# Down products of six-tile chunks from seven block products in place of eight, feed-forward chunks of 6, 6, 6 and 4 tiles

## The chip, the core and the metric

The kernel runs on one core of a Trainium2 chip. The core has a matrix engine (TensorE, PE in the profile, with its weight loads as PEld), a vector engine (DVE), a scalar engine (ACT), GpSimd (POOL), a sync engine (SP) and 16 DMA engines. Each engine works through its own list of instructions in order; they meet at semaphores. The metric is the time of one execution in microseconds. Before the change the median of three runs is 2139.5 us (2136.0 to 2141.06).

## What is computed

A streaming encoder step: 512 new frames of one stream and 64 of another (576 tokens, width 1024) pass through two layers. Each layer has a half-step feed-forward part, a mixer (a gated convolution in layer 0, chunked attention in layer 1) and a second half-step feed-forward part, each behind its own RMS norm; a last norm ends it. There are thus four feed-forward parts:

```python
D_MODEL = 1024; SEQ = 512; DEC_SEQ = 64; D_FF = 2816
def swiglu(x, w_gate, w_up, w_down):
    return (jax.nn.silu(x @ w_gate) * (x @ w_up)) @ w_down
...
for l in range(DEPTH):
    xp = xp + 0.5 * swiglu(rmsnorm(xp, ffn1_norm[l]), ffn1_w_gate[l], ffn1_w_up[l], ffn1_w_down[l])
    # mixer: conv_mixer (l = 0) or attn_mixer (l = 1), plain residual add
    xp = xp + 0.5 * swiglu(rmsnorm(xp, ffn2_norm[l]), ffn2_w_gate[l], ffn2_w_up[l], ffn2_w_down[l])
```

All data are 32-bit floats.

## The kernel before

**Layout.** Activations lie transposed: features on the 128 partitions (8 tiles of 128 for width 1024, 22 for the hidden width 2816), 576 tokens along the free axis, cut into two halves of 288. One matrix instruction multiplies a 128x128 weight tile with 288 tokens. Each operand is split into a high and a low part (`w_hi`, `w_lo` and so on), and a product takes three instructions: hi by hi, hi by lo, lo by hi.

**Phases.** The program is a list of phases (`Plan`, L93). A feed-forward part has chunks of 8, 8 and 6 hidden tiles. The first chunk is a `first` phase, which has an early stretch of plain products (`early`, PE L1403, matrix instructions at L1393) and a late stretch (`late`, L1422, matrix instructions at L1383); a later chunk is a `next` phase (`groups`, L1466). Both form gate and up tiles two by two from seven block products P1 to P7 in place of eight (Strassen's scheme in Winograd's form): j is the group of one gate and one up tile. After each chunk the hidden tiles are multiplied with the down weights: `down` (PE L1525, matrix instructions at L1500), or `last` (L1530) after the last chunk, which also prepares the next norm. There, each of the eight output tiles takes all k tiles of the chunk, 3 instructions each, for both halves: k x 6 instructions.

**Weights.** SP loads raw weight pieces from HBM into 14 staging units; POOL adds a second piece to some of them by accumulating DMAs (`add_pairs`, L610); DVE makes two further sums per group (`add_weights`, L997; instructions at L1001 and L1005). A batch of two pieces is then copied to `w_hi` by ACT (`split_batch`, instruction at L663) and its remainder made in `w_lo` by DVE (L992). There are four batch slots: batch b is split when batch b-4 has been used up, at a place that the plan fixes in the order of ACT (`split_hi`, L646) and of DVE (`split_lo`, L988).

**Order by semaphores.** `run_done` counts finished products. The fifth and sixth operand of a group start in PSUM from a copy (`seed`, ACT, L695), are read by ACT in between (`take_u2`, `take_u4`) and by DVE at the end (`take_c21`, `take_c22`, L1061 and L1056). `xadd_done` counts additions to the residual x (L1212 for a whole tile, L1217 for a half), which free PSUM banks. In `early` ACT copies each plain product out of one of four banks (L718, L721). In `last` the tiles 5, 6, 7 are made as halves (first h0, then h1), so that the norm of the first half is found while PE makes the second: squares, sums, a matrix instruction with ones (L1400), root, reciprocal (L1015), multiplication (L1027).

Of the kernel before, what the change touches and what calls it, by code (L numbers as in the profile page):

```python
# [23 lines left out]
FFN_CHUNKS = (8, 8, 6)  # L24
# [14 lines left out]
PIECE = KQ * P  # L39
W_SLOTS = 4  # L40
# [4 lines left out]
assert sum(FFN_CHUNKS) == FT  # L45

# [16 lines left out]

class Phase:
# [3 lines left out]
    def __init__(self, kind, n, k, **more):  # L68
# [8 lines left out]
        self.adds = []  # L77


class Batch:  # L80
# [4 lines left out]
    def __init__(self, first, second, width, raw, sums, ready):  # L85
        self.first, self.second, self.width, self.raw, self.sums, self.ready = first, second, width, raw, sums, ready


class Plan:
# [3 lines left out]
    def __init__(self):  # L93
        self.phases = []
        for f, norm in enumerate((0, 2, 3, 5)):
            for c, n in enumerate(FFN_CHUNKS):
                self.phases.append(Phase("first" if c == 0 else "next", n, DT, norm=norm, ffn=f, chunk=c))
                if c < len(FFN_CHUNKS) - 1:
                    self.phases.append(Phase("down", DT, n, ffn=f, chunk=c))
# [15 lines left out]
        self.rows = {8: 0, 6: 0}  # L115
# [5 lines left out]
        group = hidden = made = xadds = early = silus = 0  # L121
        for i, p in enumerate(self.phases):
            p.after = self.phases[i + 1] if i + 1 < len(self.phases) else None
            p.before = self.phases[i - 1] if i else None
            p.group, p.hidden, p.made, p.xadds, p.early, p.c11s = group, hidden, made, xadds, early, silus
            p.row = self.rows[p.k]
            self.half_batch = []
            if p.kind in ("first", "conv"):
# [12 lines left out]
                hidden += p.n  # L141
                made += p.n if p.kind == "first" else 0
                self.rows[8] += 2 * groups
                last_set = (groups - 1) % 2
            elif p.kind == "next":
                for kind, j in next_order(0, p.n, None):
                    self.product(p, kind, j, (j + first_set) % 2)
                group += p.n
                silus += p.n
                hidden += p.n  # L150
                made += p.n
                self.rows[8] += 2 * p.n
                last_set = (p.n - 1 + first_set) % 2
            elif p.kind == "down":
                pairs = (0, 1, 2, 4, 5, 6, 0, 1) if last_set == 1 else (4, 5, 6, 0, 1, 2, 4, 5)
                first_set = 1 if last_set == 1 else 0
                for m in range(DT):
                    self.tile(p, ("m", m), pairs[m], p.row + m)
                    self.free_run.append(p.run["m", m])
                xadds += DT  # L160
                self.rows[p.k] += DT
            elif p.kind == "last":
                pairs = (1, 2, 4, 5, 6, 0, 1, 2)
                for m in range(SPLIT_TILE):
                    self.tile(p, ("m", m), pairs[m], p.row + m)
                    self.free_run.append(p.run["m", m])
                for m in range(SPLIT_TILE, DT):
                    self.tile(p, ("h0", m), pairs[m], p.row + m)
# [6 lines left out]
            else:  # L175
                pairs = (4, 5, 6, 0, 1, 2)
                for r in range(3):
                    self.tile(p, ("h0", r), pairs[r], p.row + r)
# [4 lines left out]
                for t in range(1, DT):  # L183
                    for i in range(3 * t, 3 * t + 3):
                        self.tile(p, ("a", i), pairs[i % 6], p.row + i)
# [1612 lines left out]
```

## Time and profile before

| | |
|---|---|
| median of 3 runs | 2139.5 us (2136.0 to 2141.06) |
| the profiled execution, its own time | 2136.56 us |
| its span, first to last instruction | 2134.7 us |
| PE busy | 2088.5 us, 98% |
| DVE busy | 1281.3 us, 60% |
| ACT busy | 944.7 us, 44% |
| granted clock of TensorE | 0.996 of full speed over the span |

The busy times show which engine has least room. The chain of waits that ended last is 86% on PE. A matrix instruction's own duration (near 295 ns) overlaps its neighbours', so what one costs is read from how many start in a stretch.

### The profile page before, as it was taken

Reading aid. Unit: us, or ns where it says so; the run is one execution under the profiler, and the core shown is the slowest. Engines: PE = TensorE matmul, PEld = TensorE weight load, DVE = VectorE, ACT = ScalarE, POOL = GpSimd, SP = SyncE. Lnnn points to the kernel's source line nnn. Section 1 sums busy time; section 2 is a strip of 40 time slices with the busy share of each in tenths; the row PEclk is TensorE's granted clock in tenths of the full one; section 3 lists DMA queues with packets and bytes.
Section 4 is the critical chain, followed back from the end, with each engine's and each line's share of the span. In section 5 each row is a group of like instructions: output and inputs, shape, how many; then the busy total and the mean of one; then the engine's idle time right before and its main releaser. Section 6 shows DMA issues by size and latency. Waiting matters only on the chain.

```text
span 2134.7 us, 37128 instructions
## 1 busy us (share of the span) xinstructions
PE 2088.5 (98%) x15154; PEld 2011.5 (94%) x15154; DVE 1281.3 (60%) x1621; ACT 944.7 (44%) x1597; POOL 201.8 (9%) x259
## 2 busy tenths in 40 slices
PE   8999999999999999999999999999999899999997
PEld 7999999999989999999899999988888889999997
DVE  6745636578566556365764655565655467466465
ACT  5524425456445345154552533543444445244252
POOL 1101000011001010000100100100011001010000
PEclk9999999999999999999999999999999999999999
DMA  7745545457347455444554644422213247365451
GB/s 223 172 116 145 153 100 153 132 145 173 104 133 178 139 130 158 100 123 144 152 165 107 150 144 119 148 91 82 84 57 120 58 133 180 101 159 148 104 144 45
DMA packets 135416, 278.08 MB, mean 130 GB/s; under 512 B 15632, under 2 KB 20032, under 8 KB 135248
## 3 DMA queue, kind: packets, MB, share of 16 engines
q1 hardware_dynamic: 90304, 192.45, 27.7%
q0 software_dynamic: 30976, 57.53, 16.9%
q10 hardware_dynamic: 13968, 25.72, 3.5%
q8 instruction: 122, 2.00, 0.4%
q14 instruction: 46, 0.38, 0.1%
HBM read 268.55 MB, written 7.09 MB: 129 GB/s over the span
## 4 chain that ended last, share of the span: by engine, by line
PE 86%; DVE 6%; ACT 3%; DMA 3%; issue 2%; ACTq 0%; DVEq 0%; POOL 0%; POOLq 0%
PE ps L1383 39%; PE ps L1500 30%; PE ps L1393 7%; PE ps L1636 5%; DMA stage<-w 3%; ACT w_hi L663 2%; DVE w_lo L992 2%; PE ps L1614 1%; DVE neg_max L1283 1%; DVE scores L1280 1%; PE ps L1565 1%; ACT probs L913 1%; PE ps L1596 1%; DVE stage L1001 1%; PE ps L1400 0%
## 5 line engine op out<-in xcount | busy, mean ns | idle before, releaser
L663 ACT ACTIVATE w_hi<-stage 128x1024 fp32r<-128x1024 f32 (+1 forms) x446 | 464.7, 1042 | 614.8 <-PE ps L1500 387.0
L992 DVE TENSOR_TENSOR w_lo<-stage,w_hi 128x1024 fp32r<-128x1024 f32 (+1 forms) x446 | 537.5, 1205 | 284.7 <-ACT w_hi L663 280.8
L1383 PE MATMUL ps<-xa_hi,w_hi 128*128 128x288 f32 x1280 | 379.4, 296 | 2.4 <-ACT u L701 2.4
L1500 PE MATMUL ps<-hid_hi,w_hi 128*128 128x288 f32 x1664 | 380.5, 297 | 0.8 <-DVE hid_lo L1299 0.8
L1500 PE MATMUL ps<-hid_lo,w_hi 128*128 128x288 f32 x1664 | 378.1, 296 | 0.0
L1500 PE MATMUL ps<-hid_hi,w_lo 128*128 128x288 f32 x1664 | 377.9, 296 | 0.0
L1383 PE MATMUL ps<-xa_lo,w_hi 128*128 128x288 f32 x1280 | 377.9, 295 | 0.0
L1383 PE MATMUL ps<-xa_hi,w_lo 128*128 128x288 f32 x1280 | 376.8, 294 | 0.0
L1383 PE MATMUL ps<-xb_hi,w_hi 128*128 128x288 f32 x1200 | 358.4, 299 | 10.8 <-DVE up L1056 6.9
L1383 PE MATMUL ps<-xb_lo,w_hi 128*128 128x288 f32 x1200 | 354.3, 295 | 0.0
L1383 PE MATMUL ps<-xb_hi,w_lo 128*128 128x288 f32 x1200 | 353.2, 294 | 0.0
L1500 PEld LDWEIGHTS ps<-hid_hi,w_hi 128*128 128x128 f32 x1664 | 275.4, 189 | 2.6 <-issue 2.0
L1500 PEld LDWEIGHTS ps<-hid_lo,w_hi 128*128 128x128 f32 x1664 | 275.5, 189 | 0.3
L1500 PEld LDWEIGHTS ps<-hid_hi,w_lo 128*128 128x128 f32 x1664 | 275.4, 189 | 0.0
L1212 DVE SCALAR_TENSOR_TENSOR x<-ps,x 128x576 f32<-128x576 f32 x94 | 71.2, 758 | 311.4 <-PE ps L1500 311.4
L1383 PEld LDWEIGHTS ps<-xa_hi,w_hi 128*128 128x128 f32 x1280 | 240.0, 188 | 3.2 <-ACT u L701 3.0
L1383 PEld LDWEIGHTS ps<-xa_hi,w_lo 128*128 128x128 f32 x1280 | 241.1, 188 | 0.0
L1383 PEld LDWEIGHTS ps<-xa_lo,w_hi 128*128 128x128 f32 x1280 | 240.3, 188 | 0.0
L1383 PEld LDWEIGHTS ps<-xb_hi,w_hi 128*128 128x128 f32 x1200 | 225.0, 187 | 15.7 <-DVE up L1056 9.7
L1383 PEld LDWEIGHTS ps<-xb_hi,w_lo 128*128 128x128 f32 x1200 | 226.1, 188 | 0.0
L1383 PEld LDWEIGHTS ps<-xb_lo,w_hi 128*128 128x128 f32 x1200 | 225.4, 188 | 0.3
L614 POOL DMA_DIRECT2D stage<-w x100 | 86.6, 866 | 1250.2 <-DMA stage<-w 1204.4
(123 smaller groups left out, 2439.7 us busy)
## 6 DMA issues: line engine op xcount, KB each, us to landing
stage<-w SPq DMA_DIRECT2D x460, 256.0 KB, 3.8
stage<-w SPq DMA_DIRECT2D x104, 512.0 KB, 3.9
stage<-w POOLq DMA_DIRECT2D x200, 256.0 KB, 4.9
w_raw<-w ACTq DMA_DIRECT2D x80, 256.0 KB, 3.1
stage<-w SPq DMA_DIRECT2D x32, 384.0 KB, 3.8
x<-x_t SPq DMA_DIRECT2D x8, 288.0 KB, 5.0
k_t<-k_sb ACTq DMA_DIRECT2D x8, 288.0 KB, 2.1
v_t<-v_sb ACTq DMA_DIRECT2D x8, 288.0 KB, 2.5
```

The source lines that it names most:

```text
L614: pool.dma_start(stage[:, s3, :], w8[row][:, 0:PIECE], accum_op=ALU.add).then_inc(pair_added[sum3], 16)
L663: act.activation(prepared(w_hi, b), raw_of(b), ACT.Copy).then_inc(w_hi_done, 1)
L913: act.activation(probs[:, prob_slot(w, t), e, 0:width], scores[:, e, 0:width], ACT.Exp, bias=neg_max[:, w, e:e + 1], scale=1.0, accum_out= ...
L992: dve.tensor_tensor(prepared(w_lo, b), raw_of(b), prepared(w_hi, b).bitcast(F32), ALU.subtract).then_inc(w_ready, 1)
L1001: dve.tensor_tensor(stage[:, base + S2, :], stage[:, s3, :], stage[:, base + A22, :], ALU.add).then_inc(sum_done, 1)
L1212: dve.scalar_tensor_tensor(halves(x[:, m, :]), pair_banks(tile_bank(p, m)), share, halves(x[:, m, :]), ALU.mult, ALU.add).then_inc(xadd_do ...
L1280: dve.tensor_tensor(scores[:, :, 0:width], ps[:, S_BANK:S_BANK + 2, 0:width], bias[:, :, 0:width][:, :, ::-1], ALU.add).then_inc(scores_re ...
L1283: dve.tensor_reduce(neg_max[:, w, :], scores[:, :, 0:width], mybir.AxisListType.X, ALU.max, negate=True).then_inc(neg_max_done, 1)
L1383: mm = pe.matmul(ps[:, bank, 0:HALF], wt[:, b % W_SLOTS, w], xt[:, k, :], start=(start and k == 0 and n == 0), stop=(k == KQ - 1 and n == ...
L1393: mm = pe.matmul(ps[:, bank, 0:HALF], w_raw[:, b % W_SLOTS, w], raw_operand(c)[:, k, :], start=(start and k == 0), stop=(k == KQ - 1), ski ...
L1500: mm = pe.matmul(ps[:, bank + i, 0:HALF], wt[:, b % W_SLOTS, w], xt[:, k, cols(h)], start=(k == 0 and n == 0), stop=(k == p.k - 1 and n == 2))
L1636: mm = pe.matmul(ps[:, bank + i, 0:HALF], wt[:, b % W_SLOTS, w], xt[:, k % KQ, :], start=(k == 0 and n == 0), stop=(k == DT - 1 and n == 2))
```

## The change

The chunks become 6, 6, 6 and 4 hidden tiles. For the three chunks of six, `down` no longer makes eight tiles from six inputs each: inputs are kept as three pairs of tiles with seven operands per pair (B11, T1, B22, T3, T2, T4, B21), each as high and low part, and output tiles are made two by two from seven products of three pairs (9 matrix instructions each). There are four groups j, taken two at a time. The last chunk of four keeps the `last` phase as it was, with four inputs.

```diff
-FFN_CHUNKS = (8, 8, 6)
+FFN_CHUNKS = (6, 6, 6, 4)
+HIDDEN = ("B11", "T1", "B22", "T3", "T2", "T4", "B21")
+DOWN_C = (6, 0, 2, 6)
+DOWN_U = (7, 1, 3, 7)
+DOWN_E = (4, 5, 4, 5)
...
+def down_order(n):
+    order = []
+    for j in range(0, n, 2):
+        for kinds in (("P1", 0), ("P1", 1), ("P7", 0), ("P6", 0), ("P6", 1), ("P7", 1), ("P5", 0), ("P5", 1),
+                      ("P2", 0), ("P2", 1), ("P4", 0), ("P4", 1), ("P3", 0), ("P3", 1)):
+            order.append((kinds[0], j + kinds[1]))
+    return order
...
 # ACT, early: the split that follows the sixth plain product is moved behind two operand copies
-                    split_hi(p.run[kind, j])
+                    if e != 5 or p.n == DT:
+                        split_hi(p.run[kind, j])
...
                     if e == 6:
                         operand_hi(n, 5, diff_done, diffs + 3)
                         operand_hi(n, 6, diff_done, diffs + 4)
+                        if p.n < DT:
+                            split_hi(p.run[early_order(p.n)[5]])
...
 # DVE, down (for each two groups a, a + 1)
-                for m in range(DT):
-                    add_tile(p, m, 0.5)
-                    split_lo(p.run["m", m])
...
+                    for j in (a, a + 1):
+                        split_lo(p.run["P2", j])
+                    if a == 0 and p.chunk == 0:
+                        first_row_lo(p.before)
+                    for j in (a, a + 1):
+                        split_lo(p.run["P4", j])
+                    for j in (a, a + 1):
+                        dve.wait_ge(run_done, p.run["P4", j] + 1)
+                        dve.wait_ge(xadd_done, base + j - a + 3)
+                        add_to_x(x[:, 2 * j + 1, cols(0)], ps[:, DOWN_E[j], 0:HALF], 0.5)
+                    for j in (a, a + 1):
+                        split_lo(p.run["P3", j])
+                    for j in (a, a + 1):
+                        dve.wait_ge(run_done, p.run["P3", j] + 1)
+                        add_to_x(halves(x[:, 2 * j, :]), pair_banks(DOWN_C[j]), 0.5)
...
 # PE, down
+            def down_product(p, kind, j, combo, bank, start):
+                b, half = p.piece[kind, j]
+                c = HIDDEN.index(combo)
+                pe.wait_ge(w_ready, PLAN.batches[b].ready)
+                for q in range(PAIR_TILES):
+                    w = slice(half * DOWN_PIECE + q * P, half * DOWN_PIECE + (q + 1) * P)
+                    hi, lo = pair_ops[:, q, 0, c, :], pair_ops[:, q, 1, c, :]
+                    for n, (wt, xt) in enumerate(((w_hi, hi), (w_hi, lo), (w_lo, hi))):
...
+                    def p1(j):
+                        if j == 1:
+                            pe.wait_ge(c11_done, p.c11s)
+                        elif j == 2:
+                            pe.wait_ge(c12_done, p.c11s)
+                        elif j == 3:
+                            pe.wait_ge(xadd_done, p.xadds + 7)
...
 # PE, next, groups 0 and 1
-                           else pe.wait_ge(xadd_done, p.xadds - 2))
+                           else pe.wait_ge(xadd_done, p.xadds - 8))
```

ACT's `groups` keeps its line: for groups 0 and 1 the seed waits for `xadd_done` at `p.xadds - 1`, one before the last addition of the `down` phase. The operands of a pair are made by DVE (seven per two tiles, in place of two products of gate and up) and copied to their high parts by ACT, and their low parts by DVE.

Two places in the order of instructions. The first is DVE's in the `down` phase after the first chunk, from the sums at its first P2 to the last addition of the first two groups. Before the change, the same phase around its third and fourth output tile:

```order
L1034 TENSOR_TENSOR xa_lo<-xa_raw,xa_hi 128x1152 [waits x_hi_done,run_done]
L1034 TENSOR_TENSOR xa_lo<-xa_raw,xa_hi 128x1152 [waits x_hi_done]
L1212 SCALAR_TENSOR_TENSOR x<-ps,x 128x576 [waits run_done]
L992 TENSOR_TENSOR w_lo<-stage,w_hi 128x1024 [waits w_hi_done]
L1212 SCALAR_TENSOR_TENSOR x<-ps,x 128x576 [waits run_done]
L992 TENSOR_TENSOR w_lo<-stage,w_hi 128x1024 [waits w_hi_done]
```

and with the change:

```order
L1129 TENSOR_TENSOR stage<-stage 128x384 [waits raw_loaded2,pair_added2]
L1133 TENSOR_TENSOR stage<-stage 128x384 [waits raw_loaded5,sum_done]
L1120 TENSOR_TENSOR w_lo<-stage,w_hi 128x768 [waits w_hi_done]
L1162 TENSOR_TENSOR xa_lo<-xa_raw,xa_hi 128x1152 [waits x_hi_done,run_done]
L1162 TENSOR_TENSOR xa_lo<-xa_raw,xa_hi 128x1152 [waits x_hi_done]
L1129 TENSOR_TENSOR stage<-stage 128x384 [waits raw_loaded9,pair_added4]
L1133 TENSOR_TENSOR stage<-stage 128x384 [waits raw_loaded12,sum_done]
L1120 TENSOR_TENSOR w_lo<-stage,w_hi 128x768 [waits w_hi_done]
L1426 SCALAR_TENSOR_TENSOR x<-ps,x 128x288 [waits xadd_done,run_done] x2
L1120 TENSOR_TENSOR w_lo<-stage,w_hi 128x768 [waits w_hi_done]
L1426 SCALAR_TENSOR_TENSOR x<-ps,x 128x576 [waits run_done] x2
```

The addition of a finished result to x (L1212 before, L1426 now) came ahead of the split; now a split stands ahead of the last two additions, and sums and splits stand between.

The second is ACT's in the first `early` stretch, from the last two operand copies on; before the change:

```order
L688 ACTIVATE xb_hi<-xb_raw 128x1152 [waits diff_done] x2
L721 ACTIVATE est<-ps 128x288 [waits run_done]
L656 DMA w_raw<-w 128x512 [waits run_done]
L656 DMA w_raw<-w 128x512
L718 ACTIVATE est<-ps 128x288 [waits run_done]
L721 ACTIVATE est<-ps 128x288 [waits run_done]
L663 ACTIVATE w_hi<-stage 128x1024 [waits sum_done,pair_added2,run_done]
L718 ACTIVATE est<-ps 128x288 [waits run_done]
L721 ACTIVATE est<-ps 128x288 [waits run_done]
L663 ACTIVATE w_hi<-stage 128x1024 [waits sum_done,pair_added0,run_done]
```

and with the change:

```order
L754 ACTIVATE xb_hi<-xb_raw 128x1152 [waits diff_done] x2
L729 ACTIVATE w_hi<-stage 128x1024 [waits sum_done,pair_added2,run_done]
L810 ACTIVATE pair_raw<-ps 128x288 [waits run_done]
L729 ACTIVATE w_hi<-stage 128x1024 [waits sum_done,pair_added0,run_done]
L807 ACTIVATE pair_raw<-ps 128x288 [waits run_done]
L810 ACTIVATE pair_raw<-ps 128x288 [waits run_done]
L729 ACTIVATE w_hi<-stage 128x1024 [waits sum_done,raw_loaded2,run_done]
L810 ACTIVATE pair_raw<-ps 128x288 [waits run_done]
L761 ACTIVATE ps<-pair_raw 128x288 [waits c11_done]
```

Of 16 plain products' copies ten stood ahead of the first split (L663) and twelve ahead of the second; of 12 copies now seven stand ahead of the first (L729) and eight ahead of the second.

## Rows read from the trace of the kernel before

**Rows 1.** The page, busy time, share of the span and instructions of each engine.
```profile
PE 2088.5 (98%) x15154; PEld 2011.5 (94%) x15154; DVE 1281.3 (60%) x1621; ACT 944.7 (44%) x1597; POOL 201.8 (9%) x259
```

**Rows 2.** Windows, third feed-forward part: early, late, down of eight, last; busy us (instructions), clock.
```profile
1009.38:1040.82 31.44, 31.44 (x131) 24.59 (x131) 25.67 (x25) 18.27 (x31) 0.86 (x1) 1.00 0.36 118
1040.82:1106.09 65.27, 64.65 (x483) 64.20 (x482) 48.23 (x61) 36.29 (x58) 8.72 (x10) 1.00 0.73 194
1106.09:1157.27 51.18, 51.18 (x386) 51.18 (x385) 20.73 (x22) 11.29 (x11) 3.70 (x5) 1.00 0.35 86
1366.72:1406.80 40.08, 39.03 (x293) 38.73 (x292) 22.87 (x29) 22.64 (x36) 4.43 (x9) 1.00 0.34 110
```

**Rows 3.** Waits of PE: us in total, times, longest us.
```profile
PE ps L1383 <- DVE up L1056: 6.9, 11, 1.7
PE ps L1383 <- ACT ps L695: 3.9, 8, 0.5
```

**Rows 4.** Groups by line and shape: busy us, mean ns of one, idle before.
```profile
L1217 DVE SCALAR_TENSOR_TENSOR x<-ps,x 128x288 f32<-128x288 f32 x36 | 16.4, 455 | 35.8 <-PE ps L1500 35.8
L1001 DVE TENSOR_TENSOR stage<-stage 128x512 f32<-128x512 f32 x100 | 68.7, 687 | 20.5 <-DMA stage<-w 20.4
L1034 DVE TENSOR_TENSOR xa_lo<-xa_raw,xa_hi 128x1152 fp32r<-128x1152 f32 x24 | 31.6, 1353 | 0.4 <-ACT xa_hi L688 0.4
L992 DVE TENSOR_TENSOR w_lo<-stage,w_hi 128x768 fp32r<-128x768 f32 x32 | 30.6, 957 | 7.6 <-ACT w_hi L663 5.7
L663 ACT ACTIVATE w_hi<-stage 128x768 fp32r<-128x768 f32 x32 | 27.1, 846 | 52.2 <-PE ps L1500 37.8 <-PE ps L1383 14.3
```

**Rows 5.** Timeline, from a down phase to the next chunk: start us, us, engine.
```profile
307.80 1.06 ACT L663 ACTIVATE w_hi<-stage 128x1024 fp32r<-128x1024 f32 x1 [5.34 <-PE ps L1500]
307.80 0.76 DVE L1212 SCALAR_TENSOR_TENSOR x<-ps,x 128x576 f32<-128x576 f32 x1 [4.08 <-PE ps L1500]
308.89 1.23 DVE L992 TENSOR_TENSOR w_lo<-stage,w_hi 128x1024 fp32r<-128x1024 f32 x1 [0.34 <-ACT w_hi L663]
309.39 0.40 ACT L695 ACTIVATE ps<-ps 128x288 f32<-128x288 f32 x1 [0.53 <-PE ps L1383]
309.84 0.40 PE L1383 MATMUL ps<-xb_hi,w_hi 128*128 128x288 f32 x1 [0.48 <-ACT ps L695]
```

**Rows 6.** Timeline of the early stretch of the second feed-forward part.
```profile
612.19 4.04 PE L1393 MATMUL ps<-xa_raw,w_raw 128*128 128x288 f32 x16
616.55 27.32 PE L1393 MATMUL ps<-xa_raw,w_raw 128*128 128x288 f32 x112
634.41 1.06 ACT L663 ACTIVATE w_hi<-stage 128x1024 fp32r<-128x1024 f32 x1 [1.73 <-DVE stage L1001]
637.45 1.06 ACT L663 ACTIVATE w_hi<-stage 128x1024 fp32r<-128x1024 f32 x1 [0.88 <-DVE stage L1001]
638.41 0.39 ACT L718 ACTIVATE est<-ps 128x288 f32<-128x288 f32 x1
643.50 0.51 PE L1383 MATMUL ps<-xb_hi,w_hi 128*128 128x288 f32 x1
```

**Rows 7.** Timeline, ends of two last phases (before the convolution, before attention).
```profile
406.83 0.46 DVE L1217 SCALAR_TENSOR_TENSOR x<-ps,x 128x288 f32<-128x288 f32 x1 [1.55 <-PE ps L1500]
408.41 0.72 PE L1400 MATMUL ps<-sumsq,ones 128*128 128x288 f32 x2
413.31 2.63 DVE L1027 TENSOR_TENSOR xa_raw<-xa_raw,rstd 128x1152 f32<-128x1152 f32 x2
414.73 0.51 PE L1393 MATMUL ps<-xa_raw,w_raw 128*128 128x288 f32 x1
1400.63 0.72 PE L1400 MATMUL ps<-sumsq,ones 128*128 128x288 f32 x2 [1.05 <-DVE sumsq L1011]
```

**Rows 8.** Start of the program: PE's timeline, then windows with the granted clock.
```profile
14.54 4.87 PE L1393 MATMUL ps<-xa_raw,w_raw 128*128 128x288 f32 x12 [3.97 <-DVE xa_raw L1027]
14.00:18.00 4.00, 3.46 (x9) 2.52 (x10) 3.50 (x6) 2.67 (x8) 0.00 (x0) 0.66 0.86 264
```

**Rows 9.** DMA issues: queue, count, KB each, median us to landing.
```profile
stage<-w SPq DMA_DIRECT2D x460, 256.0 KB, 3.8
stage<-w SPq DMA_DIRECT2D x32, 384.0 KB, 3.8
```

More of the change, by code:

```diff
@@ L77, in __init__ @@
         self.adds = []
+        self.paired = kind in ("first", "next") and self.chunk < len(FFN_CHUNKS) - 1
 class Batch:
-    def __init__(self, first, second, width, raw, sums, ready):
+    def __init__(self, first, second, width, raw, sums, ready, piece=None):
+        self.piece = piece
         self.first, self.second, self.width, self.raw, self.sums, self.ready = first, second, width, raw, sums, ready
@@ L98, in __init__ @@
                 if c < len(FFN_CHUNKS) - 1:
[L99 removed]
+                    self.phases.append(Phase("down", DOWN_GROUPS, n, ffn=f, chunk=c))
                 else:
@@ L120, in __init__ @@
         self.sets = 0
-        group = hidden = made = xadds = early = silus = 0
+        group = seeds = pairs = hidden = made = xadds = early = silus = 0
         for i, p in enumerate(self.phases):
@@ L241, in product @@
         base = 7 * part
-        if kind == ("P1" if p.kind == "next" or j >= DT else "P6"):
+        if p.kind == "down":
+            if kind == "P1" and part == 0:
+                self.load_down_pair(p, j)
+        elif kind == ("P1" if p.kind == "next" or j >= DT else "P6"):
             s3 = A11 if kind == "P6" and j // 2 % 2 else S3
@@ L271, in product, with load_down_pair @@
             self.add_piece(p, kind, j, base + piece, sums)
+    def load_down_pair(self, p, j):
+        for piece, row, second in ((A11, 0, 0), (S3, 0, 0), (A21, 1, 0), (A12, 0, 1), (A22, 1, 1)):
+            for part in range(2):
+                self.load_piece(p, 7 * part + piece, 2 * (j + part) + row, second)
+        for kind, piece, second in (("P7", S3, 0), ("P5", A21, 1)):
+            for part in range(2):
+                p.piece["s3", j + part] = S3
+                sums = p.piece.setdefault(("sums", j + part), {})
+                sums[kind] = self.add_second(p, 7 * part + piece, part + (2 + part if kind == "P7" else 0),
+                                             2 * (j + part) + 1, second)
     def tile(self, p, name, pair, row):
@@ L635, in _ @@
             for p in PHASES:
-                if p.kind in ("first", "next", "conv"):
+                if p.kind in ("first", "next", "conv", "down"):
                     add_pairs(p)
@@ L773, in late @@
                     take_c12(j)
+                    if p.kind == "first" and j == p.n - 1:
+                        last_tile_hi(p)
                     split_hi(p.run["P3", j])
@@ new lines, in pair_lo, with tile_lo @@
+            def pair_lo(p, q, first, end, hi, done=1):
+                dve.wait_ge(pair_hi_done, PAIR_HI * (p.pairs + q) + hi)
+                part = flat(pair_raw[:, q, 1, first:end, :])
+                dve.tensor_tensor(flat(pair_ops[:, q, 1, first:end, :]), part,
+                                  flat(pair_ops[:, q, 0, first:end, :]).bitcast(F32),
+                                  ALU.subtract).then_inc(pair_ready, done)
+            def tile_lo(p, j):
+                q = j // 2
+                if not p.paired:
+                    hidden_lo(p, j, up[:, j % 2, :])
+                elif j % 2 == 0:
+                    pair_lo(p, q, 0, 2, 2)
+                else:
+                    pair_lo(p, q, 2, 7, 5, 3)
```

416 lines of the change are left out of this document (306 added, 110 removed).

## The prediction, as it was put on record before the run

> **What bounds the kernel.** I read the busy times first: PE is busy 98% of the span, DVE 60%, ACT 44% [rows 1]. The windows of one feed-forward part say the same by stage: early, late, down and last keep PE busy all through, at full clock, and the waits of PE by releaser are only a few microseconds [rows 2, 3]. So the count of matrix instructions sets the time, and any wait that PE gets anew comes on top.
>
> Two prices on PE. The down of eight has 384 matrix instructions (8 x 8 x 6) in 51.18 us: 0.1333 us each [rows 2]. Plain products: 112 records from 616.55 to 643.50, 0.2406 us each [rows 6], and eight records make one plain product, 1.925 us; a split product of 12 instructions is 1.60 us, a new down product of 9 is 1.20 us.
>
> **A. Down products.** Before, per feed-forward part: 384 + 384 + 6 x 48 = 1056 instructions. After: 3 x 28 x 9 + 4 x 48 = 948. That is 108 fewer, 432 in four parts: **-57.6 us**.
>
> By the Trainium skill (TensorE: Matmul & The Clock Gate, section "Wait — 56ns, not 53.3ns?") back-to-back matmuls at the high clock start N / 2.4 GHz plus 2.5 ns apart, 122.5 ns for 288 columns. The trace has 133.3 ns [rows 2], which decides; with the page's figure A would be an estimated -52.9 us and B +23.5 us.
>
> **B. More split products for gate and up.** Two tiles move from the first chunk to later ones. A tile there has seven split products, in the first chunk two plain and five split ones. Before: 8 x 5 + 14 x 7 = 138 split ones, after 6 x 5 + 16 x 7 = 142: four more per part, 6.4 us, **+25.6 us** in all.
>
> **C. Early stretch, 12 plain products in place of 16.** By count it would take 23.6 us in place of 31.3 (643.50 - 612.19) [rows 6]. But ACT's first two weight splits wait for DVE's sums, which follow the norm's chain on DVE; that chain starts with the stretch and does not get shorter. They ran at 634.41 and 637.45 [rows 6]. Now the ninth product's copy stands behind the second split, and PE's twelfth product needs it. The copy would end where the row's does, at 638.41 + 0.39 = 638.8, PE starts the twelfth at 638.9 and ends at 640.8. Behind the copy ACT has a copy, a split, a copy and the seed, 0.41 + 1.06 + 0.39 + 0.41 less overlaps of 0.09, until 640.9. The late stretch starts at about 641.0, 28.8 us after the start: 2.5 us saved per part, **-10 us**, and not 30.8. Bounds: -30.8, and nothing saved.
>
> **D. A new wait at P1 of group 3.** It needs bank 6, freed by the seventh addition to x. Take PE at 0 when a down starts. P1 of group 3 would start after 15 products, at 18.0. P3 of group 1 ends at 16.8. In front of the seventh addition DVE has a split that waits for this end: 0.20 until ACT starts (307.60 to 307.80), ACT 0.85, DVE 0.96, then the addition 0.76, with an overlap of 0.09 [rows 4, 5]. So it ends no sooner than 19.6: floor 1.6 us. DVE is also behind. From P5's end at 9.6: two u copies and the split on ACT to 10.97, the split on DVE to 11.96, two additions of 0.76 (0.68 each with overlap) to 13.3, two sums of 384 (estimated 0.55 from 0.687 for 512) to 14.4, ACT and DVE split to 15.7, two sums to 16.7; ACT's split waits for the first of these and runs 16.15 to 17.0, DVE's to 18.0, two half additions of 0.455 to 18.75, the split to 19.6, the seventh addition to 20.3. PE waits 2.35 us. After the first chunk two operand remainders of 1.35 us stand in between as well [rows 4]: the same count gives 23.0 and a wait of 5.1 us. Per part 5.1 + 2.35 + 2.35 = 9.8: **+39.2 us**. Behind the waiting P1 all of PE's list stands. Floor 19 us, if DVE has no backlog; above, 60 if the sums wait for loads too.
>
> **E. The seed after a down.** Before, the seed follows P1 of the next chunk and PE waits about 0.65 us (0.48 in the row, the rest start-up of the first instruction) [rows 3, 5]. Now it also waits for the last but one addition, which stands behind a 1024-wide split. From the end of the down: 0.20 + 1.06 + 1.23 + 0.76 + 0.40 and the hand-overs, 3.7 us; DVE's backlog, in which sums wait for a piece whose unit is only then freed, makes it 4.05. PE has P1's 1.60 us to do: wait 2.45. There are three per part in place of two: 3 x 2.45 - 2 x 0.65 = 6.05, **+24.2 us**; floor 20.
>
> **F. End of last.** The last phase now has 24 instructions per tile in place of 36, and 12 per half tile in place of 18. But the chain from the last h0 tile (its end 406.63, the addition at 406.83) through L1400 at 408.41 to the multiplication at 413.31, whose first half ends near 414.67 and releases PE at 414.73 [rows 7], is DVE's and ACT's; h1 tiles of 4.8 us in place of 7.2 no longer fill it. So 2.4 us of A do not arrive, in each of four parts; before attention, where PE already waits 1.05 us for the sum [rows 7], 1.9 more: **+11.5 us**. Bounds 0 and 20.
>
> **G. Late stretch.** For two tiles PE takes 16 us. DVE has five splits of 1.14 (with overlap), four sums, four reads of 0.37 and now the pair's operands: two tiles of 0.76 + 0.76 become 576 + 288 + 576 in the first and 288 + 864 + 288 + 288 + 1440 in the second, some 5.6 us in place of 3.1. That is 15.6 of 16 us. PE waits for DVE's L1056 already, 6.9 us in all [rows 3]. I take 1.5 us more per part, **+6 us**; bounds 0 and 20.
>
> **H. The clock.** Before PE's first plain product it idled 3.97 us, and in 14 to 18 us the granted clock was 0.66 on average, so at its lower level (1.2 of 2.4 GHz) for much of it [rows 8]. I let the four waits of 5.1 us in D do the same, at (1 - 0.66) x 4 = 1.4 us each: **+5.6 us**.
>
> Operands ready at a down's start I cost at nothing: the first products use tiles made earlier, and the last tile's T3 would be ready 2.2 us after the start, against 2.4 needed. Should DVE be late by a microsecond there, twelve downs cost up to 12 us.
>
> **Sum.** -57.6 + 25.6 - 10.0 + 39.2 + 24.2 + 11.5 + 6.0 + 5.6 = +44.5. From the profiled execution's 2136.56 us: **2181 us**. The median of the runs is 2.9 us above that execution, within what I leave open.
>
> **Rivals.**
> - *The additions come in time* (the other side). If DVE reaches the seventh addition before 18.0 and the last but one before the seed is due, D, E and H go: 44.5 - 39.2 - 24.2 - 5.6 plus one more seed of 0.65 per part = -21.9, **2115 us**. It decides at 18.0 after a down's start. For it: DVE is only 60% busy. Against it: the order, split ahead of addition, whose split waits for an end at 16.8. Chance 0.07; if C and F came in full too, the time would be 2077, which I count within these.
> - *Floors.* DVE has no backlog: D 19, E 20, F 7, G and H nothing, which leaves -57.6 + 25.6 - 10 + 46 = +4, **2141 us**. For it: my sums of DVE take each operation one after another. Against: DVE has some 13.8 us of work per 16.8, more after the first chunk. Chance 0.13, a third of it within 0.2%.
> - *Loads late.* Each two groups now take ten loads and four accumulating ones in 16.8 us. A piece of 384 KB lands in 3.8 us, as one of 256 KB does [rows 9]; so pieces of 192 KB hardly land sooner, while the units are freed 7.2 us ahead of use in place of 9.6. If sums then wait 1 to 2 us in each of 24 such stretches: +25 us, **2206 us**. For it: DVE's sums wait 20.4 us for loads already [rows 4]. Against: by my count these land 2 us before they are needed. Chance 0.13.
>
> By the Trainium skill (DMA: Bandwidth & Descriptors, section "Anatomy of one DMA — SWDGE (gpsimd) path") a DMA takes a fixed 2 us plus its bytes at 436 GB/s; the trace's 3.8 us for either size agrees that size hardly counts. By it the third rival would be likelier than I have it.
>
> **Chances.** Forecast 0.67, rivals 0.07, 0.13, 0.13. A measurement of this kernel can tell 0.2%, 4.3 us, from no change. Faster 0.08, same 0.04, slower 0.88. The range from 2146 to 2210 takes the forecast's own bounds, the upper rival and the top of the second's.
>
> **What would show it.** D: PE's wait for DVE's addition line, 12 times, 5 us after first chunks, some 2.4 after others. E: 12 waits for ACT's seed near 2 us in place of 8 of 0.5. C: early stretches of 28 to 29 us, PE waiting on ACT before the twelfth product. F: a wait of near 2 us before the first plain product. A: 432 fewer matrix instructions at 0.133 us. It is wrong if the waits at P1 of group 3 are short, so that PE stays 98% busy.

## The result, and the profile after

The changed kernel takes **2257.65 us** (median of 4 runs, 2252.68 to 2259.15) against 2137.75 us (4 runs, 2134.36 to 2141.06) of the kernel before on the same chip: 1.0552 times as long, 95% interval 1.0531 to 1.0573. The forecast was 2181 us with a range up to 2210: slower, as said, but by 116 us in the spans of the profiled runs (2134.7 and 2250.9) and not by 44.5.

The page after, busy time of each engine, answers to [rows 1]:

```profile
PE 2079.4 (92%) x14786; PEld 1990.8 (88%) x14786; DVE 1564.1 (69%) x2137; ACT 1111.2 (49%) x1905; POOL 285.4 (13%) x355
```

PE is nearly as busy as before (2079.4 against 2088.5 us) with 368 fewer instructions, and its share fell from 98% to 92%. The waits of PE, us in total, times, longest us; before, the two lines of [rows 3] were the seed (3.9 us) and DVE's read in the split groups (6.9 us):

```profile
PE ps L1645 <- DVE x L1426: 39.6, 12, 5.2
PE ps L1623 <- ACT ps L761: 24.5, 12, 2.5
PE ps L1623 <- ACT u_u L775: 21.7, 22, 1.1
PE ps L1633 <- ACT pair_raw L807: 20.6, 4, 6.6
PE ps L1623 <- DVE up L1184: 16.4, 19, 1.7
PE ps L1653 <- DVE sumsq L1139: 14.5, 6, 5.8
PE ps L1633 <- DVE xa_raw L1155: 7.2, 3, 4.0
```

From the top: a down's fourth group (step D), the seed after a down (E), ACT's read of P5's sum, which P3 needs (u4; not in the forecast), the copy of a plain product (C), DVE's read of P7's sum, which P4 needs (c22; G), and the end of a last phase (F, two lines). The windows of the third feed-forward part, the columns as in [rows 2] (busy us and instructions of PE, PEld, DVE, ACT, POOL, then clock, DMA share, GB/s), in the order early, late, down, next, down, next, down, next of four tiles, last:

```profile
1069.20:1099.60 30.40, 25.69 (x98) 19.51 (x99) 25.70 (x25) 16.21 (x26) 0.00 (x0) 0.91 0.29 91
1099.60:1152.80 53.20, 49.97 (x363) 48.78 (x361) 42.25 (x58) 29.36 (x47) 10.42 (x12) 0.99 0.68 163
1152.80:1193.30 40.50, 35.34 (x252) 34.97 (x253) 30.15 (x43) 20.21 (x31) 6.10 (x8) 0.96 0.61 143
1193.30:1265.50 72.20, 68.00 (x507) 67.29 (x506) 54.27 (x73) 38.02 (x59) 10.45 (x12) 1.00 0.60 150
1265.50:1301.40 35.90, 33.53 (x254) 33.30 (x253) 26.68 (x39) 18.27 (x29) 6.93 (x8) 1.00 0.68 159
1301.40:1375.80 74.40, 69.79 (x507) 68.85 (x506) 54.11 (x73) 37.80 (x59) 10.39 (x12) 0.98 0.60 147
1375.80:1411.70 35.90, 33.53 (x254) 33.30 (x254) 25.93 (x40) 18.21 (x29) 6.93 (x8) 1.00 0.66 158
1411.70:1459.20 47.50, 45.02 (x338) 44.79 (x337) 29.59 (x39) 22.45 (x37) 3.45 (x4) 1.00 0.50 130
1459.20:1491.50 32.30, 28.01 (x196) 27.47 (x195) 20.89 (x29) 21.73 (x36) 4.42 (x9) 0.95 0.43 134
```

Two things are to be seen. The helpers have less slack: DVE is busy 25.7 of 30.4 us in early and 42.3 of 53.2 in late, where it was 25.7 of 31.4 and 48.2 of 65.3 [rows 2]. And the granted clock is below 1.00 in five of nine windows, where before it was 1.00 in all four.

For all four parts I added up the distances between PE's first instructions of consecutive stages (the last one up to PE's last instruction), and set the forecast beside them (before, plus the change in the count of instructions times 0.1333 us, plus the terms):

| stage, us over four parts | before | forecast | after | after less forecast |
|---|---|---|---|---|
| early | 127.2 | 117.2 | 124.7 | 7.5 |
| late | 264.7 | 206.7 | 214.4 | 7.7 |
| downs | 409.5 | 448.0 | 459.4 | 11.4 |
| products of later chunks | 633.1 | 746.9 | 788.3 | 41.4 |
| last | 163.4 | 123.7 | 126.8 | 3.1 |

These 71.1 us are the miss, but for some 0.5 outside the four parts. What the low clock costs is counted from the distances between PE's instructions in stretches at the lower level (1.2 of 2.4 GHz), each less what it is at the upper one: 39.4 us after (347 distances) and 2.3 us before (22).

### The profile page after: what moved, and what is told of

Its sections match the earlier page's. It is cut to its first block and busy times, and to the rows that moved or that the text cites. A ratio compares the mean times of both kernels' runs of the same rounds, so it can differ in the third digit from the quotient of the medians.

```text
span 2250.9 us, 38384 instructions
## 1 busy us (share of the span) xinstructions
PE 2079.4 (92%) x14786; PEld 1990.8 (88%) x14786; DVE 1564.1 (69%) x2137; ACT 1111.2 (49%) x1905; POOL 285.4 (13%) x355
## 3 DMA queue, kind: packets, MB, share of 16 engines
q1 hardware_dynamic: 116800, 204.00, 28.8%
## 5 line engine op out<-in xcount | busy, mean ns | idle before, releaser
L1120 DVE TENSOR_TENSOR w_lo<-stage,w_hi 128x1024 fp32r<-128x1024 f32 (+2 forms) x558 | 619.5, 1112 | 371.0 <-ACT w_hi L729 369.4
L729 ACT ACTIVATE w_hi<-stage 128x1024 fp32r<-128x1024 f32 (+2 forms) x558 | 538.1, 967 | 428.3 <-DVE stage L1129 249.1
L683 POOL DMA_DIRECT2D stage<-w x296 | 257.0, 909 | 1614.1 <-DMA stage<-w 1586.6
L1645 PE MATMUL ps<-pair_ops,w_hi 128*128 128x288 f32 x2016 | 416.7, 303 | 39.9 <-DVE x L1426 39.6
L1623 PE MATMUL ps<-xa_hi,w_hi 128*128 128x288 f32 x1344 | 404.5, 301 | 24.7 <-ACT u_u L775 21.7
L1623 PE MATMUL ps<-xb_hi,w_hi 128*128 128x288 f32 x1200 | 363.6, 303 | 40.9 <-ACT ps L761 24.5
L1645 PEld LDWEIGHTS ps<-pair_ops,w_hi 128*128 128x128 f32 x2016 | 333.9, 195 | 44.2 <-DVE x L1426 42.4
L1645 PE MATMUL ps<-pair_ops,w_lo 128*128 128x288 f32 x1008 | 302.6, 300 | 0.0
L1645 PEld LDWEIGHTS ps<-pair_ops,w_lo 128*128 128x128 f32 x1008 | 196.4, 195 | 0.0
L1633 PE MATMUL ps<-xa_raw,w_raw 128*128 128x288 f32 x512 | 136.6, 429 | 27.8 <-ACT pair_raw L807 20.6
L1633 PEld LDWEIGHTS ps<-xa_raw,w_raw 128*128 128x128 f32 x512 | 101.8, 200 | 59.3 <-ACT pair_raw L807 22.4
L1753 PE MATMUL ps<-hid_hi,w_hi 128*128 128x288 f32 x512 | 130.8, 302 | 3.0 <-DVE hid_lo L1278 2.3
```

The source lines that it names most:

```text
L683: pool.dma_start(stage[:, unit, 0:part.stop - part.start], {8: w8, 6: w6}[k][row][:, part], accum_op=ALU.add).then_inc(pair_added[pair_sum ...
L729: act.activation(prepared(w_hi, b), raw_of(b), ACT.Copy).then_inc(w_hi_done, 1)
L1120: dve.tensor_tensor(prepared(w_lo, b), raw_of(b), prepared(w_hi, b).bitcast(F32), ALU.subtract).then_inc(w_ready, 1)
L1623: mm = pe.matmul(ps[:, bank, 0:HALF], wt[:, b % W_SLOTS, w], xt[:, k, :], start=(start and k == 0 and n == 0), stop=(k == KQ - 1 and n == ...
L1633: mm = pe.matmul(ps[:, bank, 0:HALF], w_raw[:, b % W_SLOTS, w], raw_operand(c)[:, k, :], start=(start and k == 0), stop=(k == KQ - 1), ski ...
L1645: mm = pe.matmul(ps[:, bank, 0:HALF], wt[:, b % W_SLOTS, w], xt, start=(start and q == 0 and n == 0), stop=(q == PAIR_TILES - 1 and n == 2 ...
```

## The experiments

Each run is compared with the kernel before on the same chip; medians of before were 2136.7 to 2139.2 us. The gains below are against the changed kernel's 2257.65 us, which was measured apart from them, so a difference under some 5 us says nothing. Waits and stages come from one profiled execution of each run, and can differ by some us from what the medians say. The edits are shown shortened: a line can stand for several of the kernel's. "The clock's cost" is always counted as above.

### Clock: fill

```diff
+ if (kind, j, q, n) == ("P1", 2, PAIR_TILES - 1, 2):
+     fill(bank, 20 if p.chunk == 0 else 9)
+ if j == 0: fill(1, 8)                 # next chunk, ahead of the seeded P6
+ if e == 11 and p.n < DT: fill(5, 20)  # early, ahead of the twelfth plain product
```

> Edit: the kernel after, with matrix instructions of 128 columns on constants that PE issues where it would otherwise idle: 20 ahead of the fourth group's first product in downs after the first chunk (9 in the other downs), 8 ahead of the seeded product of every next chunk, 20 ahead of the twelfth plain product. They are made to be shorter than the wait they fill, so every wait for DVE or ACT ends when it did. Theory (each of these waits also takes TensorE's clock down, and this is the main thing I sized too small): the lower-clock stretches outside the start and the end go, mean clock 0.99, and about 35 us come back: 2222 us. Rival (a fallen clock costs the 5.6 us that I gave it, the rest of the miss is work of ACT and DVE): 2250 us or more.

The first of these stands in the middle of a product, in the same bank on other columns, and x comes out wrong; why was not looked into, and the run counts for its time alone. Measured: **2231.7 us**, ratio 1.0442 (1.0426 to 1.0457), 26 us less; mean granted clock 0.992 in place of 0.974. What the low clock costs fell from 39.4 to 9.0 us. The waits that were filled are no longer shown as idle, and some behind them grew, u4's from 21.7 to 26.7 us and c22's from 16.4 to 19.3:

```profile
PE ps L1628 <- ACT u_u L775: 26.7, 24, 2.4
PE ps L1628 <- DVE up L1184: 19.3, 17, 1.7
PE ps L1628 <- ACT ps L761: 6.0, 12, 2.3
PE ps L1652 <- DVE x L1426: 5.6, 12, 0.7
```

So the clock was a term of 37 us, not of 5.6, and 30 of it are had back by instructions that compute nothing. 26 reach the end of the program.

### Order of DVE in a down: add_first, row, ready_row

```diff
  # add_first: both additions of P3 ahead of the splits at P3
+ for j in (a, a + 1): dve.wait_ge(run_done, p.run["P3", j] + 1); add_to_x(...)
  for j in (a, a + 1): split_lo(p.run["P3", j])
- for j in (a, a + 1): dve.wait_ge(...); add_to_x(...)
```

> Edit: the kernel after, with DVE's two last additions of each pair of down groups ahead of the weight split that they stood behind. Theory: PE's wait at the fourth group's first product (39.6 us in 12) and at the seed after a down (24.5 in 12) nearly go, and with them the clock's falls there, some 25 us: 2170 to 2180 us. Rival (DVE is too busy in a down; the split comes 1.5 us later and PE then waits for weights instead): half of it, 2215 us, with new waits of PE for the remainder line of the weights.

Measured: 2224.3 us, ratio 1.0409 (1.0393 to 1.0424). The waits at the fourth group fell only from 39.6 to 29.2 us, those for the seed to 17.2. My theory was half wrong: the last split was not the only thing ahead of the seventh addition.

```diff
  # row: the operand remainders of the first down
- if a == 0 and p.chunk == 0: first_row_lo(p.before)   # ahead of the splits at P4
+ if a == 2 and p.chunk == 0: first_row_lo(p.before)   # ahead of the splits at P5
```

> Edit: the kernel after, with DVE's two operand remainders (1.35 us each) of the first down moved from ahead of the second products' splits of groups 0 and 1 to the same place of groups 2 and 3, behind their first additions. Theory (after first chunks DVE's backlog is these two): the four waits of 5.1 us at the fourth group's first product become 2.4 us, and the clock falls for half as long: 10.8 + some 4 = 15 us, 2243 us. Rival (the backlog comes from sums that wait for loads, and the remainders fill time that DVE would wait anyway): under 4 us.

Measured: 2255.0 us, ratio 1.0542 (1.0514 to 1.057): nothing that can be told. The longest wait at the fourth group did fall from 5.2 to 2.8 us (30.3 in all), but the seed's rose from 24.5 to 30.2 and u4's from 21.7 to 25.2. By stages the downs fell from 459.4 to 451.0 us and the products of later chunks rose from 788.3 to 796.2: what was taken out of the downs was paid behind them.

```diff
  # ready_row: row, and
  for j in (a, a + 1): split_lo(p.run["P2", j])
+ additions of P4 (a, a + 1); addition of P3 (a)
  for j in (a, a + 1): split_lo(p.run["P4", j])
- additions of P4 (a, a + 1)
+ addition of P3 (a + 1)
  for j in (a, a + 1): split_lo(p.run["P3", j])
- additions of P3 (a, a + 1)
```

> Edit: as the run before, and DVE's last four additions of each two groups stand ahead of the sums and splits at the fourth and third products, each where its data is ready. With only the last two additions ahead of the last split the run of that gave 2224 us and left 29.2 us of waits there, DVE being held by the split that ACT had to do first. Theory (the order of DVE alone makes these waits, it has the time): the waits for the addition line fall below 8 us in 12 and those for the seed below 12, 2185 us. Rival (DVE's time is full in a down: 26.7 of 35.9 us are busy, and the rest is latency that only moves): sums and splits come late instead, and PE waits for weights; 2215 us.

Measured: **2190.5 us**, ratio 1.0237 (1.0193 to 1.0281), 67 us less. The wait for the addition is gone from the list, and the first down of the third part, which had taken 40.5 us, runs without a gap and at full clock, though DVE is still busy 27.9 us in it, against 30.2 (the window's columns as above):

```profile
1122.99:1156.50 33.51, 33.51 (x252) 33.40 (x253) 27.86 (x41) 18.06 (x30) 6.12 (x8) 1.00 0.69 164
```

The twelve downs fell from 459.4 to 399.9 us. So step D, 39.6 us of waits, was 59.5 with what went with it, the clock above all, and all of it came from the order on DVE (row alone had taken 8.4 of it out of the downs and lost it behind them): what it had to take over before the seventh addition was splits that wait for ACT, which waits for sums. The seed's waits stayed, at 25.8 us. In that kernel's successor comb (below) ACT's timeline shows why (start, us, engine, idle before it and what ended that):

```profile
1367.41 2.95 ACT L729 ACTIVATE w_hi<-stage 128x1024 fp32r<-128x1024 f32 x3 [4.37 <-DMA stage<-w]
```

Three splits stand ahead of the seed, and the first waited for a load. In the changed kernel itself it was not so: there ACT's seed waited for DVE's addition all 12 times, 25.1 us in all, as step E says.

### Pair operands: nextu4, next2, thin

```diff
  # nextu4, ACT:  seed, u2, [copy of pair operands moved] c11, u4, + tile_hi(p, j - 1)
  # nextu4, DVE:  splits P6, P2, + tile_lo(p, j - 1), split P5, c22, split P7
  # next2, DVE:   splits P6, P2, P5, c22, + tile_lo(p, j - 1), split P7
```

> Edit: the kernel after, with ACT's copy of the pair operands (up to 128x1440) behind the two reads that PE waits for in the groups of next chunks, and DVE's remainder of it one split later. Theory: PE's waits for the read before the seventh product (21.7 us in 22) fall below 6 us: 2240 us. Rival (DVE's remainder then delays its read before the fourth product, PE's wait of 16.4 us for that line grows by as much): 2255 us.

Measured: 2267.4 us, ratio 1.061 (1.0589 to 1.0631), slower by some 10 us, and by more than the rival had it. Its mechanism held: the waits for u4 fell to 9.6 us, those for c22 rose from 16.4 to 37.8.

> Edit: the kernel after, with ACT's copy of the pair operands behind its reads, and DVE's remainder of it behind DVE's read of the sixth product in place of ahead of it. With the remainder one split later the waits for ACT's read fell from 21.7 to 9.6 us, and those for DVE's read rose from 16.4 to 37.8. Theory (only DVE's place of the remainder made those): waits for both lines together 38.1 us before, now under 20: 2238 us. Rival (the operations of pair operands do not fit into the group whatever their order): 2255 us or more.

Measured: 2247.2 us, ratio 1.05 (1.0478 to 1.0521). Waits for c22 are 21.7 and for u4 6.5 us, 28 together in place of 38. The place of the remainder matters, but 10 us are half of what I expected. What had held PE in the changed kernel is seen where one of those 22 waits is. ACT, then DVE, then PE:

```profile
1224.21 1.06 ACT L729 ACTIVATE w_hi<-stage 128x1024 fp32r<-128x1024 f32 x1 [2.47 <-DVE stage L1129]
1225.18 1.39 ACT L784 ACTIVATE pair_ops<-pair_raw 128x1440 fp32r<-128x1440 f32 x1
1226.47 0.39 ACT L939 ACTIVATE pair_raw<-ps 128x288 f32<-128x288 f32 x1
1226.76 0.40 ACT L775 ACTIVATE u_u<-ps 128x288 f32<-128x288 f32 x1
...
1221.57 1.06 DVE L1230 TENSOR_TENSOR pair_raw<-pair_raw 128x864 f32<-128x864 f32 x1
1222.55 0.45 DVE L1239 TENSOR_TENSOR pair_raw<-pair_raw,up 128x288 f32<-128x288 f32 x1
1223.04 0.46 DVE L1242 TENSOR_TENSOR pair_raw<-pair_raw 128x288 f32<-128x288 f32 x1
1223.41 0.68 DVE L1129 TENSOR_TENSOR stage<-stage 128x512 f32<-128x512 f32 x1
1226.67 1.66 DVE L1248 TENSOR_TENSOR pair_ops<-pair_raw,pair_ops 128x1440 fp32r<-128x1440 f32 x1
...
1227.21 0.40 PE L1623 MATMUL ps<-xa_hi,w_hi 128*128 128x288 f32 x1 [1.12 <-ACT u_u L775]
```

DVE's three operations on the odd tile hold up the sums at 1223.41; ACT's split waits 2.47 us for these; behind it stand a copy of 1.39 us, the gate's copy and then u4, for which PE has been waiting 1.12 us.

```diff
  # thin, in pair_hi and in pair_lo
+ end = first + 1
```

> Edit: the kernel after, in which ACT's copies to pair operands and DVE's remainders of them are one operand wide (288 columns in place of up to 1440), and the down products read those operands alone: the hidden layer's combinations are wrong, every instruction and every wait is there. Theory (the waits that I gave no price in the next chunks come from ACT standing in the 1.39 us copy and DVE in the 1.66 us remainder): PE's waits for ACT's read before the seventh product go from 21.7 to under 5 us, those for DVE's read from 16.4 to about 7, as before the change: 2257 - 26 = 2230 us, with waits at the fourth group and at the seed as they were. Rival (those waits come from the loads and sums, not from pair operands): above 2250 us.

Measured: 2232.8 us, ratio 1.0436 (1.0405 to 1.0468), 25 us less where 26 were expected. The waits for the fourth group and the seed are as they were, u4's fell from 21.7 to 5.2 us, as the theory had it; c22's only from 16.4 to 13.8, where it had 7:

```profile
PE ps L1648 <- DVE x L1428: 39.4, 12, 5.1
PE ps L1625 <- ACT ps L761: 25.7, 12, 2.8
PE ps L1625 <- DVE up L1185: 13.8, 15, 2.4
...
PE ps L1625 <- ACT u_u L775: 5.2, 19, 1.3
```

By stages the products of later chunks fell from 788.3 to 772.9 us and late from 214.4 to 211.0. The two profiled executions are only 15.4 us apart (2250.9 and 2235.5), the medians 25, so the stages tell where the time went and the medians how much it is. For this work in the later chunks my forecast had no price.

### The early stretch: early, thin_early

```diff
  # early, ACT: splits freed at the 6th, 8th and 10th product
- behind the copies of the 7th, 8th and 10th product
+ behind the copy of the 9th; behind the copy of the 11th and the first seed (two)
```

> Edit: the kernel after, with ACT's first weight splits in the early stretch placed behind its copies of the plain products (the one that stood before the ninth product's copy goes behind it, the next two behind the copy after the eleventh product and the first seed). Theory: PE's wait before the twelfth plain product (20.6 us in 4) goes with the clock's fall there; the late stretch starts when the first remainder is ready, 5.5 us sooner per part: 22 us, 2236 us. Rival (the late stretch is set by DVE's sums and splits, which move by nothing): the wait moves to the first split products, 2250 us.

Measured: 2257.2 us, ratio 1.0549 (1.0525 to 1.0573): the same time. The plain products now run through (20.3 us behind the sum of the norm, in place of 25.9), and the late stretches are 5.5 to 6.7 us longer: a new wait for DVE's remainders of weights (4.9 us), u4's from 21.7 to 35.0 us. The rival was right: the early end of the plain products only moved the wait.

```diff
  # thin_early, DVE: operand remainders of norms 0, 2, 3, 5 (not B11, B21)
+ width = HALF      # in place of KQ * HALF
```

> Edit: the kernel after, in which DVE's five operand remainders of the early stretch are 288 columns wide in place of 1152 (0.45 us in place of 1.35), and the products use the rounded operand in place of them: less exact. ACT's order is as it was. Theory (DVE's chain sets when ACT's first split can run, and so the wait before the twelfth plain product): 4.5 us less on the chain, the wait goes from 4.9 to about 0.5 in each of four parts and the late stretch follows: 18 us less and 1 to 2 us of clock each, 2235 us. Rival (ACT's order or the loads set it): above 2250 us.

Measured: 2240.3 us, ratio 1.0466 (1.0443 to 1.0489), 17 us less. The early stretches fell from 124.7 to 104.2 us. ACT's order was not touched, and the first of the two splits ahead of the ninth product's copy came 18.6 us after PE's start in place of 22.3: DVE's chain sets it, as step C says.

### Together, and the eighth product: comb, seedfirst, thin_sf, eighth, ready_eighth, sf_fill

comb is ready_row with next2's edit.

> Edit: the kernel after with the edits of the two runs before it (all additions where ready, remainders of the first down late, pair operands behind the reads). Theory: the gains add, 2257 - 72 - 19 = 2166 us; the clock's lower stretches outside start and end fall from some 100 us to under 40. Rival (the waits only change place): 2200 us.

Measured: 2181.7 us, ratio 1.0194 (1.0158 to 1.0229), 76 us less. The gains do add: ready_row's 67 and next2's 10 make some 77. The 2166 us of the theory came from the larger gains that were expected of those two.

```diff
  # seedfirst: comb, and at the end of a down
  DVE: + additions of P4 and P3, then splits at P2, P4, P3
  ACT: split at P2, + seed of the next chunk, then splits at P4, P3
```

> Edit: the kernel comb (2182 us), and at the end of a down DVE's last four additions ahead of the three 1024-wide splits, and ACT's seed ahead of the last two of them. Theory (the 24.2 us of waits for the seed come from the split that waits for a load, in front of the additions and the seed): they fall below 10 us, with the clock's falls there: 2155 us. Rival (the splits are then late for the fifth and seventh product): 2175 us or more.

Measured: **2158.1 us**, ratio 1.0091 (1.0073 to 1.0109); the seed's waits are 6.1 us:

```profile
PE ps L1636 <- DVE up L1188: 24.7, 36, 2.0
PE ps L1646 <- ACT pair_raw L807: 20.6, 4, 6.6
PE ps L1666 <- DVE sumsq L1143: 14.9, 7, 5.8
PE ps L1646 <- DVE xa_raw L1159: 7.2, 3, 4.0
PE ps L1636 <- ACT ps L761: 6.1, 12, 0.8
```

This is the fastest of the runs that leave nothing of the computation out, 99.5 us better than the changed kernel and still 0.9% slower than the one before.

> Edit: the run before, with matrix instructions of 128 columns on constants in PE's wait before the twelfth plain product (20, 4.8 us in each of four parts) and before the seed after a down (6). No wait ends sooner. Theory (a wait of 4.8 us costs the clock another 1.5 to 2.5 us): 10 us less than the run before. Rival: within 3 us of it.

Measured: 2159.2 us, ratio 1.0092 (1.0074 to 1.0111): no gain. The cost of the low clock fell from 13.6 to 7.1 us and the early stretches from 125.5 to 119.9, but the stages behind the filled waits grew, late from 216.9 to 220.1 us and the later chunks' products from 747.6 to 752.6. Where DVE and ACT set the pace behind a wait, a fast PE only waits for them later. Such instructions were worth 26 us in the changed kernel, where many of them stood in downs.

> Edit: the same narrow pair operands in the kernel seedfirst (2158 us). Theory: its 24.7 us of waits for DVE's read fall to about 8; 2140 us, level with the kernel before, so that with the order mended the whole loss of the change is the pair operands' work and the early and last stretches. Rival: 2150 us or more, the rest lies in early, late and last whatever the operands cost.

Measured: 2138.3 us, ratio 0.9996 (0.9982 to 1.001): level with the kernel before, 20 us less than seedfirst; waits for c22 11.8 us.

```diff
  # eighth: every down group accumulates its last product twice
  p4(a); p4(a + 1)
+ eighth(a); eighth(a + 1)
  p3(a); p3(a + 1)
```

> Edit: the kernel after, in which every down group does an eighth block product again: its last product is accumulated twice, so x gets a wrong share of it. These are the 432 matrix instructions that seven products save in twelve downs, 57.6 us of PE. ACT, DVE and the loads do what they did. Theory (the order of ACT and DVE sets when the fourth group may start, not PE): each wait there, 5.2 and 2.5 us, takes up the 2.4 us of two products ahead of it, 12 x 2.4 = 28.8 us, and the clock falls less, some 10 us; 2257 + 57.6 - 29 - 10 = 2277 us, so of A's 57.6 us only some 20 arrived. Rival (A arrived in full): 2315 us.

Measured: 2273.5 us, ratio 1.0637 (1.0616 to 1.0658), near the theory's 2277. 57.6 us more of matrix instructions cost 16 us. The wait at the fourth group took up 17 of the rest (39.6 us before), and the clock fell less (mean 0.982 in place of 0.974):

```profile
PE ps L1645 <- DVE x L1426: 22.4, 12, 2.8
```

> Edit: the same eighth product in the kernel whose additions stand where ready (2190 us, and no wait at the fourth group). Theory: there A arrives in full, so that this is 2190 + 57.6, less what the waits at the seed take up of it (they end by ACT and loads, some of which come earlier against PE; 0 to 10 us): 2240 to 2248 us. Rival (the waits take it up here as well): under 2225 us.

Measured: 2219.7 us, ratio 1.0382 (1.0357 to 1.0407), 29 us more than ready_row: the rival, under 2225, was right, and A does not arrive in full here either. The waits for the seed fell from 25.8 to 5.8 us and the cost of the low clock from 24.8 to 13.3; together 31.5 us, about the 28 that are missing. With a product more per group, the loads at the end of a down come in time.

## Why the prediction was wrong, step by step

**A, B: right in what they count.** 368 fewer records on PE, of which 432 and 128 less and 192 more; a down that runs through takes 33.5 us for 252. But A's gain reached the end only as far as the helpers let it: some 16 us of 57.6 (eighth), 29 with DVE's additions in their mended order (ready_eighth).

**D: right in place and length.** Forecast 39.2 us of waits with 5.1 after first chunks and 2.35 after others; measured 39.6 in 12 waits, 5.2 the longest. At 1176.19 PE resumes behind the seventh addition, for which DVE did two half additions, a split and then this one, one after another:

```profile
1172.04 1.58 ACT L729 ACTIVATE w_hi<-stage 128x768 fp32r<-128x768 f32 x2 [2.26 <-DVE stage L1129]
1173.79 0.81 DVE L1426 SCALAR_TENSOR_TENSOR x<-ps,x 128x288 f32<-128x288 f32 x2
1174.52 0.95 DVE L1120 TENSOR_TENSOR w_lo<-stage,w_hi 128x768 fp32r<-128x768 f32 x1
1175.39 1.41 DVE L1426 SCALAR_TENSOR_TENSOR x<-ps,x 128x576 f32<-128x576 f32 x2
1176.19 0.85 PE L1645 MATMUL ps<-pair_ops,w_hi 128*128 128x288 f32 x2 [5.16 <-DVE x L1426]
```

**E: right.** 12 waits, 24.5 us in the view and 2.13 us each for most with the start-up, where 2.45 were forecast. Loads set the seed only once the additions stood earlier (comb, seedfirst).

**H: the step that failed most.** I gave four waits of 5.1 us a price of 1.4 each. By stages the low clock cost 14.5 us in downs, 11.9 in later chunks, 7.2 in early, 2.7 in late and 1.5 in last, 37.8 in the four parts; before it was 1.6. That is 30.6 us more than the forecast. It fell behind waits of 2.13 and 2.53 us, and of 4.7 in early, too, and one fall costs more than the 4 us of [rows 8] had shown, for the stretch is longer: 6.80 us at 0.50 in this window around the first part's wait in early:

```profile
42.80:49.60 6.80, 4.57 (x11) 3.43 (x12) 3.85 (x5) 3.64 (x8) 0.76 (x1) 0.50 0.30 95
```

By the Trainium skill (TensorE: Matmul & The Clock Gate, section "Terms") the penalty is about the throttled time times the share of clock that is missing. The trace has 121.2 us at the low level after and 18.9 before, so an estimated 51 us by that rule; 37 were measured: in part of those stretches PE was still waiting, as in the window above, where it is busy for 4.57 of 6.80 us.

**Operands, costed at nothing: the other step that failed.** I looked only at whether the operands were ready when a down starts. They were. But ACT and DVE make them in the groups of later chunks, ahead of the read that PE waits for. The later chunks' products were 29.5 us over the forecast besides the clock. The waits there that had no price are u4's, 24.7 us with PE's start-up, and c22's, 4.2 (21.4 and 3.0 in the view); the seed's were 3.0 below the forecast. The width of the operands alone is 25 us of the median (thin) and takes 15.4 from this stage. The rest is left open: thin kept the number and order of the added operations, and no run took those away or changed the loads, for which DVE waits 32.8 us where it waited 20.4.

**C: right in mechanism, wrong in what follows.** The wait came before the twelfth product, in each part. A stretch of 28.8 us was forecast, 30.2 measured in the three parts after the first. The clock's fall behind that wait makes 5.6 of the 7.5 us missed in four parts (7.2 us against 1.6 before). early and thin_early show that DVE's chain is behind it, and that the order on ACT tried in early saves nothing.

**G: too small.** Besides its count and the clock, late took 11.0 us more than before where 6 were forecast; in the view the waits for c22 and u4 there are 12.1 us (10 waits) after 5.3 (8). **F: right.** 11.5 us were forecast, and its two lines of waits grew from 11.8 to 21.7.

Summed: clock 30.6, later chunks besides it 29.5, late 5.0, downs 2.5, early 1.9, last 1.6, together the 71.1 us. The loads rival at 2206 us was the nearest in time, but by luck: DVE's waits for loads grew by 12 us and not by 25. The other rival, the additions in time, has a slip in its best case: with C and F in full it comes to 2082 us, and to 2077 only if G goes as well. The range was too narrow at the top because it let the clock fall in four places, though the forecast itself held 28 new waits of over 2 us.

Why even the mended order does not win: thin_sf shows 20 us of pair operands that nothing covers, and seedfirst still has the waits of early (20.6 us), late (13.4 of c22's 24.7) and last (22.1, where the kernel before has 11.8). Fewer instructions per product leave PE less time than DVE's and ACT's chains need there. That no better order exists for late and last was not tried.

## What to carry to other kernels

When an edit takes work from a PE that is 98% busy, list what each other engine must finish in the shortened time, in its own order, at every place where the work is made and not only where it is used. The helpers' order, not their busy share (DVE 69%), decided here, and another order of additions, pair operands and a seed gave back 99.5 of the 119.9 us lost.

Price every new wait with the clock behind it: here a wait of over 2 us cost its own length and often 1.5 to 2.5 us more (37 us over the forecast's 28 such waits is 1.3 each). But fill a wait only where PE sets the pace behind it.

To find out what a saving is worth, put it back as work without effect: where 57.6 us of instructions cost 16, the bound is elsewhere.

## What the runs showed of the hardware

Two waits of the same length (2.37 us idle) at the same place of a down ended at 239.5 and 1285.9 us. The windows of the 3.4 to 3.8 us with the wait, and of the 4.7 us behind it:

```profile
236.00:239.40 3.40, 1.15 (x9) 0.92 (x7) 3.16 (x6) 1.34 (x3) 0.87 (x1) 1.00 0.22 72
239.50:244.20 4.70, 4.68 (x24) 4.68 (x25) 1.59 (x2) 1.14 (x2) 0.86 (x1) 0.64 0.66 165
1282.00:1285.80 3.80, 1.51 (x12) 1.28 (x10) 3.40 (x7) 1.71 (x3) 0.86 (x1) 1.00 0.21 73
1285.90:1290.60 4.70, 4.70 (x35) 4.70 (x36) 1.55 (x2) 1.99 (x4) 0.86 (x1) 1.00 0.72 170
```

PE was busy 1.15 and 1.51 us ahead, and behind it the clock was 0.64 once and 1.00 once: 24 instructions against 35 in the same 4.7 us. Of the eight downs after second and third chunks, each with such a wait, five took 37.4 to 37.6 us and three 35.9 to 36.0. So after a wait of this length a fall may come or not, and the length of the wait does not decide it; what does was not settled.
